# A hybrid decoder step: the turns of the parameter and state rows, moved behind three passes of a head tile

## The reference

```
h = rmsnorm(x, g_mix_pre)
proj = h @ w_in            # q, k, v, rnn input, gelu gate, merge gates
o_attn = moba_chunked(...) # block-sparse attention, T5 bias; samples read a paged cache
xc = sum(xpad[:, j:j + T] * conv_w[j] for j in range(CONV_W)) + conv_b
hseq, h_last = rglru(xc, h_past, w_r, b_r, w_i, b_i, lam)
merged = sigmoid(gate_a) * (o_attn @ w_pa) + sigmoid(gate_r) * (hseq * gelu(gb) @ w_pr)
x = x + rmsnorm(merged @ w_out, g_mix_post)
x = x + rmsnorm((silu(g_) * u_) @ w_down, g_ffn_post)
```

## Time and profile before

| | us |
|---|---|
| median of 3 runs | 762.58 |
| lowest, highest | 762.55, 763.48 |
| the profiled execution | 762.54 |
| its span in the trace | 760.7 |
| PE busy in it | 752.1 (99%) |
| DVE busy | 519.5 (68%) |
| ACT busy | 376.2 (49%) |
| POOL busy | 116.4 (15%) |

### The profile page before, as it was taken

How to read it: one execution, slowest core, us unless ns; L and a number is a source line. 1 busy time by engine, 2 the same in 40 slices (tenths; PEclk the granted TensorE clock), 3 DMA queues, 4 the chain that set the end, 5 groups by cost and what they waited for, 6 DMA issues and landing times.

```text
span 760.7 us, 16105 instructions
## 1 busy us (share of the span) xinstructions
PE 752.1 (99%) x5903; PEld 712.3 (94%) x5903; DVE 519.5 (68%) x823; ACT 376.2 (49%) x670; POOL 116.4 (15%) x228
## 2 busy tenths in 40 slices
PE   8999999999999999999999999999999999999996
PEld 6998899898898999987899999999999999999996
DVE  7446838656665575784569887787777899764644
ACT  7334625534733642343466555455554568454442
POOL 6602102010120110003000000000000000453650
PEclk9999999999999999999999999999999999999999
DMA  9645555545544315516561333223332312424274
GB/s 264 167 113 118 155 129 124 152 107 115 149 114 107 88 56 171 166 59 184 172 184 39 112 110 107 83 86 110 110 105 84 87 50 72 138 73 134 69 227 135
DMA packets 185065, 91.77 MB, mean 121 GB/s; under 512 B 52454, under 2 KB 177850, under 8 KB 185020
## 3 DMA queue, kind: packets, MB, share of 16 engines
q1 hardware_dynamic: 178958, 82.69, 39.4%
q0 software_dynamic: 4880, 8.13, 4.0%
q10 hardware_dynamic: 1182, 0.35, 0.2%
HBM read 82.37 MB, written 6.81 MB: 117 GB/s over the span
## 4 chain that ended last, share of the span: by engine, by line
PE 97%; DMA 1%; POOL 1%; DVE 0%; DVEq 0%; issue 0%; ACT 0%; POOLq 0%
PE ps L1082 34%; PE ps L1471 28%; PE ps L1588 7%; PE ps L1365 6%; PE ps L1573 5%; PE ps L1535 4%; PE ps L1439 3%; PE ps L1288 2%; PE ps L1189 1%; PE ps L1203 1%; PE ps L1221 1%; DMA strow<-in_state_h_dram 1%; PE ps L1263 1%; PE ps L1174 1%; PE ps L1373 1%; PE ps L1234 1%
## 5 line engine op out<-in xcount | busy, mean ns | idle before, releaser
L1082 PE MATMUL ps<-xin_hi,w_hi 128*128 128x272 f32 x544 | 117.0, 296 | 0.0
L1082 PE MATMUL ps<-xin_hi,w_lo 128*128 128x272 f32 x544 | 112.5, 288 | 0.0
L1082 PE MATMUL ps<-xin_lo,w_hi 128*128 128x272 f32 x544 | 112.3, 288 | 0.0
L1082 PEld LDWEIGHTS ps<-xin_hi,w_hi 128*128 128x128 f32 x544 | 84.8, 188 | 8.1 <-issue 7.6
L2248 DVE TENSOR_TENSOR w_lo<-w_raw,w_hi 128x1024 fp32r<-128x1024 f32 (+1 forms) x46 | 55.9, 1215 | 51.4 <-ACT w_hi L1663 50.2
L1082 PEld LDWEIGHTS ps<-xin_lo,w_hi 128*128 128x128 f32 x544 | 85.4, 188 | 0.0
L1082 PEld LDWEIGHTS ps<-xin_hi,w_lo 128*128 128x128 f32 x544 | 85.0, 189 | 0.0
L648 POOL DMA_DIRECT2D ytok<-yz x48 | 33.8, 710 | 306.5 <-DVE yz L2809 306.5
L1663 ACT ACTIVATE w_hi<-w_raw 128x1024 fp32r<-128x1024 f32 (+1 forms) x47 | 49.2, 1049 | 49.0 <-PE ps L1082 39.6
L1471 PE MATMUL ps<-xq_lo,b_hi 128*128 128x272 f32 x160 | 46.6, 292 | 0.0
L1471 PE MATMUL ps<-xq_hi,a_lo 128*128 128x272 f32 x160 | 46.4, 290 | 0.0
(11 more groups left out here) (397 smaller groups left out, 2134.4 us busy)
## 6 DMA issues: line engine op xcount, KB each, us to landing
w_raw<-in_w_in_dram SPq DMA_DIRECT2D x68, 256.0 KB, 3.5
g_raw<-in_w_gate_up_dram SPq DMA_DIRECT2D x40, 256.0 KB, 3.8
u_raw<-in_w_gate_up_dram SPq DMA_DIRECT2D x20, 256.0 KB, 3.1
e_raw<-in_w_gate_up_dram SPq DMA_DIRECT2D x20, 256.0 KB, 4.3
raw_p<-in_w_down_dram SPq DMA_DIRECT2D x24, 192.0 KB, 2.6
kc<-in_cache_k_dram SPq DMA_DIRECT2D x64, 64.0 KB
vc<-in_cache_v_dram SPq DMA_DIRECT2D x64, 64.0 KB
raw<-in_w_down_dram SPq DMA_DIRECT2D x12, 320.0 KB, 3.1
```

The lines of the kernel that those rows point to most:

```text
L1082: mm = e.matmul(ps[:, bank + h, 0:HT], wt[:, kw, :], xt[:, kx, h * HT:h * HT + HT], start=first and wt is wh and xt is xh, stop=last and ( ...
```

## The change

The five turns of the parameter and state rows, with their wait for `par_in`, are written behind the three passes of weight tile 0 over the first half, in place of between the first of them and the second. No other engine's instructions are touched, and none is added or removed.

```
             e.wait_ge(xt_hi, 4)
             head_pass(0, 0, w_hi[0], xin_hi, first=True, k0=KD // 2)
+            split_ready(0)
+            head_pass(0, 0, w_lo[0], xin_hi)
+            e.wait_ge(xt_lo, 4)
+            head_pass(0, 0, w_hi[0], xin_lo, last=True)
             e.wait_ge(par_in, 176)
             e.transpose(ps[:, 2, 0:56], prow[:, :], ident[0:56, 0:56]).then_inc(small_T, 1)
             for f in range(PAIRS):
                 mm = e.transpose(ps[:, 2, 64 + 32 * f:96 + 32 * f], strow[:, f * P:f * P + P], ident[0:32, 0:32])
             mm.then_inc(small_T, 1)
-            split_ready(0)
-            head_pass(0, 0, w_lo[0], xin_hi)
-            e.wait_ge(xt_lo, 4)
-            head_pass(0, 0, w_hi[0], xin_lo, last=True)
             x_T(2)
             e.wait_ge(hi_done, 2)
             e.wait_ge(small_c, 2)
```

More of the change, by code:

```diff
@@ L1302, in _ @@
             mm.then_inc(small_T, 1)
[L1303 to L1306, removed]
             x_T(2)
```

## The result

| | before | changed |
|---|---|---|
| median, 13 runs each, us | 763.12 | 765.20 |
| lowest, highest, us | 762.55, 765.10 | 763.93, 766.25 |
| ratio | | 1.0026 (95%: 1.0019 to 1.0033) |
| the profiled execution, its span, us | 762.54, 760.7 | 766.22, 764.4 |

The account below looks back on a forecast made before the run. PE was taken as the bound, busy 752.1 of 760.7 us. A 0.12 us gain ahead of x_T(2) was outweighed by VectorE's lateness, net +0.65 at x_T(TT): 762.54 + 0.65 = 763.2 us, range 762.4 to 764.1.

Parts of the forecast that it names:

- likeliest course: Prologue: VectorE late by about 0.7 us and PE by 0.5 to 0.8, taken as +0.65; chance 0.72.
- The term that it called decisive: VectorE's two copies out of bank 2 wait for the moved turns: VectorE 0.74 us late, x_T(TT) about +0.65.
- What is late next: Behind x_T(TT): later VectorE steps are in time, next weight tile's lo part with 0.57 us of room; nothing added.
- kept gain: Rival: VectorE's delay does not reach PE and the shorter wait's 0.12 us is kept, 762.4 us; chance 0.07.
- taken back: Rival: a later wait that doesn't follow PE takes back some of the 0.65, 762.7 to 763.0 us; chance 0.13.
- The w_lo pass did not wait as long as the turns had: Rival: w_lo pass waits as long as the turns did, everything to the copies 0.20 later, 763.4 us; chance 0.03.
- The clock: Rival: TensorE falls to 1.2 GHz from x_T(2) until the third pass, 766.7 us; chance 0.03.
- Parameters that land late: At the turns: a landing 0.5 us later costs the kernel before 0.5 us and the changed one nothing.

Follow-up runs that it names:

- the second trace: The changed kernel as it is, run and traced once more: 764.78 us, 1.0021 of before; its traced execution took 763.26 us.
- the two held kernels: The changed kernel and the kernel before, each with GpSimd's bias copies waiting for the lo part of the next weight tile: 763.55 and 762.66 us.
- The added delay on VectorE alone: Kernel before, turns in their old place, two fills added on VectorE behind the two copies out of bank 2: 765.05 us, 1.0016 of before.
- the hold: A wait added on GpSimd: bias copies start only when the lo part of the next weight tile is done; on the changed kernel 763.55 us.
- the hold alone: The kernel before with only the added wait on GpSimd's bias copies: 762.66 us, 0.9993 of before.
- the two kernels with late tiny steps: Kernel before with two 1024-column fills on VectorE ahead of the tiny parameter steps, GpSimd's bias copies free or made to wait: 767.60 and 764.69 us.
- first trace of the changed kernel: The profiled execution of the changed kernel in the first measurement: 766.22 us, span 764.4.
- late steps with the hold: Kernel before with two 1024-column fills ahead of VectorE's tiny parameter steps, and GpSimd's bias copies made to wait: 764.69 us, 1.0016 of before.
- late steps without the hold: Kernel before with two 1024-column fills ahead of VectorE's tiny parameter steps, GpSimd unchanged: 767.60 us, 1.0050 of before.

## Why the prediction was wrong

**The likeliest course was forecast step by step, and it is what an execution of the changed kernel without the collision does.** Against the second trace, whose first pass starts 0.07 us late:

| step | forecast, us | measured, us |
|---|---|---|
| idle ahead of the w_lo pass | 0.22, for GpSimd | 0.24, for GpSimd |
| `prm` copy on VectorE | 15.26 | 15.36 |
| turn of `prow` | 14.60 | 14.70 |
| x_T(2) | 15.15 | 15.25 |
| x_T(3) | 17.13 | 17.22 |
| x_T(TT) | 19.64 | 19.72 |
| idle ahead of it, for VectorE | 0.6 | 0.46 |
| loop (L1082) | 27.7 | 27.77 |
| span | 761.3 to 761.4 | 761.5 |
| time of that execution | 763.2 | 763.26 |

The term that it called decisive, VectorE's copies stuck behind the moved turns, is right, and its size too: the two held kernels stand 0.89 us apart in the medians and 0.72 in the lowest runs, where it said 0.65 with bounds of 0.5 to 0.8. The added delay on VectorE alone brought the same wait of 0.46 us at x_T(TT). That it came out at 0.65 is in part luck of the one trace that it was worked out from. From the start of the first head pass to that of the last it takes 15.50 to 15.52 us in the three traces of the changed kernel, with the hold or without; with the turns in their old place it took 14.87 in the trace used, but 15.22 where the parameters landed late (the hold alone) and 14.74 to 14.78 where they landed earlier and no wait is listed at the turn of `prow` (the two kernels with late tiny steps). So the place costs 0.3 to 0.8 us, by the landing.

**The step that failed is the one headed "What is late next".** It asked whether each later VectorE step would be done before TensorE wants it, found 0.57 us of room at L2255, and stopped. It took the durations of VectorE's steps as given, wherever they are moved to. It also said that GpSimd's queue holds nothing that waits for the turns. That is true, and misses the point: GpSimd's copies were released by their DMAs at 26.3 whatever VectorE did, and VectorE moved towards them. The tiny steps ended 0.95 us ahead of the first copy; 0.74 of that was used up by the forecast's own sum, and the scatter of the landings is larger than what was left, 0.21: in the six traces without the hold the copies start at 25.95 to 26.39. What the runs showed in the place of "nothing is added" is 1.2 us, by which the hold makes the changed kernel faster. Had the GpSimd row at 26.29 stood beside the VectorE row at 25.25, this would have been a rival with a price of its own.

The Trainium skill states the mechanism, in "SBUF — State Buffer", section "SBUF: two separate sides": VectorE and GpSimd share a pair of ports under an exclusive lock, taken by a VectorE instruction with two SBUF inputs against a GpSimd instruction that reads SBUF, and the one that starts second waits for the other's end. These traces agree: the tiny steps end 0.02 us behind the copy that they began under, and 0.16 us become 0.56. The port itself is not to be seen in a trace; that the two exclude each other is. The rows of the kernel before had the sign of it, a lo part of 1.50 us beside one of 1.22.

**The range was too narrow by its own argument.** It was built around the profiled execution (762.54), which is as low as the lowest of the 13 runs (762.55); their median is 763.12. The 0.7 us that it adds for scatter comes out of no row: the highest run before, 763.48, lay 0.9 us above the median of 762.58. With 0.9 the range would end at 764.3, still below 765.20. Nor was a difference of this size beyond what can be told: the ratio of 1.0026 has an interval of 1.0019 to 1.0033. And a sum with a threshold in it needs both sides of the threshold in the range.

**The rivals.** The kept gain didn't come, as said, and nothing of the 0.65 was taken back before the loop (27.77, where 27.7 was forecast). The w_lo pass did not wait as long as the turns had (0.24 us, not 0.42). The clock did not fall in either trace of the changed kernel, for all its thirteen turns in a row (1.00 from 16 to 21 us in the first, from 14 to 21 in the second); where an experiment idled TensorE for 3.18 us, it did fall, and cost about 1.0 us or somewhat more. Parameters that land late cost the kernel before 0.35 us in one trace (0.79 us of idle time ahead of the turn). In the first trace of the changed kernel the state rows took 7.9 us from issue to landing, where 5.83 had been the time before, and no wait stands at the turns; but everything was late there. The effect is small against the rest.

**What stays open.** That the runs without a trace collide is concluded from the 1.2 us that the hold takes off them, not seen in them. Why nine of eleven do, where the traced one missed by 0.16 us, is not shown: a run without a trace tells no landings. Of the four traces with late steps and no hold three collide: the first of the changed kernel, which had the late first weight as well, and the two of the kernel before with added delay.

## What to carry to other kernels

When a change makes an engine late, look not only at who waits for it but at what it will now run beside: VectorE steps with SBUF inputs and GpSimd copies excluded each other here, and in a chain of tiny steps each one that began under a copy of 0.67 us paid 0.4 us. Where an engine's stream holds a step that waits for another engine, moving what it waits for moves everything queued behind it, so move it no further than to where the reader comes to it of itself (here behind the second pass, not the third). A sum that ends within a few tenths of a microsecond of such an overlap has two outcomes, and both belong in the range.

## What the runs showed of the hardware

A VectorE step of 4 columns took 0.16 us alone and 0.56 to 0.57 under a GpSimd copy of 256 columns (0.67), ending 0.02 behind it; in the first trace of the changed kernel four steps and four copies alternated in this way until the copies were through. It went the other way as well: with VectorE's 1.22 us step in first, GpSimd's four copies took 3.31 us in place of 2.54, one of them 1.48. TensorE kept its full clock after idle times of 1.25 and 1.7 us (changed kernel, first trace) and of 1.52 us (late steps with the hold), and was at half of it after 3.18 us (late steps without the hold: 0.50 in the first two microseconds, 1.00 again from 35 us on).
